# Depthwise convolution of a conformer layer: taps shared out anew over four engines, input weights in chunks of 128 features with their gates

## The reference, cut to what matters

```python
def conformer_conv(h, w_pw1, b_pw1, w_dw, b_dw, ln_g, ln_b, w_pw2, b_pw2):
    a, gate = jnp.split(h @ w_pw1 + b_pw1, 2, axis=-1)      # 1024 -> 2 x 1024
    u = a * jax.nn.sigmoid(gate)
    dw = lax.conv_general_dilated(                          # 31 taps, causal, per feature
        u, w_dw[:, None, :], window_strides=(1,), padding=((CONV_WIDTH_2 - 1, 0),),
        dimension_numbers=('NWC', 'WIO', 'NWC'), feature_group_count=D_MODEL) + b_dw
    ...                                                     # layer norm of dw, silu
    return z @ w_pw2 + b_pw2
```

## Time and profile before

| what | us |
|---|---|
| median of 3 runs | 1363.0 |
| lowest and highest run | 1354.35, 1363.15 |
| the profiled execution's own time | 1360.02 |
| its span in the trace | 1358.2 |
| PE busy in the span | 1295.7 (95%) |
| DVE busy | 920.8 (68%) |
| ACT busy | 712.7 (52%) |
| POOL busy | 43.3 (3%) |

### The profile page before, as it was taken

The page is one execution under the profiler, slowest core; times in us unless marked ns, Lnnn a source line. Parts: engine busy times, 40 slices in busy tenths (PEclk is TensorE's granted clock), DMA queues, the critical chain, the costliest instruction groups (busy, mean ns, idle before and its releaser), DMA issues.

```text
span 1358.2 us, 17587 instructions
## 1 busy us (share of the span) xinstructions
PE 1295.7 (95%) x7034; PEld 1106.1 (81%) x7034; DVE 920.8 (68%) x1270; ACT 712.7 (52%) x1074; POOL 43.3 (3%) x80
## 2 busy tenths in 40 slices
PE   6999999999999878999999999999998998999997
PEld 5998678888888767888888877888888996788886
DVE  4967565676666676666667756666666895776665
ACT  5865344554445654555445544544446664544443
POOL 0000000000000400000000000000000000000000
PEclk9999999999999889999999999999999998999999
DMA  6453235455555311455555543555554321455551
GB/s 241 156 186 124 94 110 200 155 187 187 186 186 169 143 62 47 144 213 186 187 186 187 198 152 126 184 186 189 187 188 166 109 79 62 155 187 186 202 186 62
DMA packets 30785, 215.17 MB, mean 158 GB/s; under 512 B 3552, under 2 KB 3808, under 8 KB 5488
## 3 DMA queue, kind: packets, MB, share of 16 engines
q1 hardware_dynamic: 30704, 214.05, 44.0%
HBM read 212.99 MB, written 1.05 MB: 158 GB/s over the span
## 4 chain that ended last, share of the span: by engine, by line
PE 89%; DVE 5%; ACT 3%; issue 1%; POOL 0%; DMA 0%; SPq 0%; POOLq 0%; ACTq 0%; DVEq 0%
PE pb L428 24%; PE pb L399 15%; PE pb L401 14%; PE pb L400 14%; PE pb L430 12%; PE pb L913 3%; PE pb L405 2%; DVE wlo L1432 2%; ACT arena L980 1%; DVE arena L1436 1%; ACT both L980 1%; DVE both L1445 1%; PE pb L754 1%; ACT whi L976 1%; PE pb L531 0%
## 5 line engine op out<-in xcount | busy, mean ns | idle before, releaser
L1432 DVE TENSOR_TENSOR wlo<-raw,whi 128x2048 fp32r<-128x2048 f32 (+2 forms) x201 | 453.3, 2272 | 233.8 <-ACT whi L976 233.7
L428 PE MATMUL pb<-both,whi 128*128 128x512 f32 x1408 | 498.4, 398 | 6.5 <-DVE both L1445 4.3
L976 ACT ACTIVATE whi<-raw 128x2048 fp32r<-128x2048 f32 (+2 forms) x201 | 379.3, 1893 | 39.9 <-PE pb L401 35.6
L430 PE MATMUL pb<-both,wlo 128*128 128x256 f32 x1408 | 394.9, 280 | 0.0
L428 PEld LDWEIGHTS pb<-both,whi 128*128 128x128 f32 x1408 | 264.4, 188 | 73.3 <-issue 5.1
L399 PE MATMUL pb<-whi,both 128*128 128x512 f32 (+1 forms) x754 | 298.0, 395 | 11.2 <-DVE both L1445 5.3
L401 PE MATMUL pb<-whi,both 128*128 128x512 f32 (+1 forms) x754 | 294.1, 390 | 0.0
L400 PE MATMUL pb<-wlo,both 128*128 128x512 f32 (+1 forms) x754 | 293.5, 389 | 0.0
L430 PEld LDWEIGHTS pb<-both,wlo 128*128 128x128 f32 x1408 | 265.8, 189 | 1.4
L980 ACT ACTIVATE arena<-pb 128x256 f32<-128x256 f32 (+1 forms) x248 | 103.5, 426 | 252.1 <-PE pb L430 171.8
L399 PEld LDWEIGHTS pb<-whi,both 128*128 128x128 f32 x754 | 142.7, 189 | 44.7 <-issue 8.6
(11 more groups left out here) (117 smaller groups left out, 913.6 us busy)
## 6 DMA issues: line engine op xcount, KB each, us to landing
raw<-d_ws SPq DMA_DIRECT2D x196, 1024.0 KB, 4.9
raw<-d_ws SPq DMA_DIRECT2D x3, 768.0 KB, 4.3
arena<-d_c SPq DMA_DIRECT2D x1, 1060.0 KB, 4.8
xt<-d_x SPq DMA_DIRECT2D x2, 512.0 KB, 4.2
arena<-d_rows SPq DMA_DIRECT2D x2, 512.0 KB, 5.2
out<-arena SPq DMA_DIRECT2D x2, 512.0 KB, 2.6
raw<-d_ws SPq DMA_DIRECT2D x1, 640.0 KB, 3.8
c<-d_c SPq DMA_DIRECT2D x1, 385.0 KB, 5.4
```

Source lines behind the costliest of these rows:

```text
L428: e.matmul(b[:, :], wh[:, k, fs], both[:, k, :], start=k == 0, stop=k == 7, skip_group_check=True)
L430: m = e.matmul(b[:, 256:512], wl[:, k, fs], ahi[:, k, :], start=False, stop=k == 7, skip_group_check=True)
L976: e.activation(whi[:, n % NH, 0:width(n)], raw[:, n % NR, 0:width(n)], ACT.Copy).then_inc(*sig("act.hi", f"hi{n}"))
L1432: e.tensor_tensor(wlo[:, n % NH, 0:width(n)], raw[:, n % NR, 0:width(n)], f32(whi[:, n % NH, 0:width(n)]), ALU.subtract).then_inc(*sig("dv ...
```

## The change

- The `pw1` weights are laid out by the host so that each chunk p holds 128 values and the 128 gates that belong to them. Tile p can be gated as soon as chunk p is done; the sigmoid, the gating and tap 0 are done tile by tile.
- The 30 other taps of a tile are shared by three: PE 6, 7, 8, 8, 8, 8, 11, 15 (71 in all), DVE 15, 13, 12, 12, 12, 12, 10, 10 (96) and a third share of 9, 10, 10, 10, 10, 10, 9, 5 (73). For these, ACT makes the product `up * w` (128x256, SBUF to SBUF): the first of a tile into `part` (three buffers), the others into `prod` (`NX` = 6 buffers), and POOL adds each `prod` to `part` (65 tensor-tensor adds, both inputs in SBUF, each waiting for the one before). DVE adds `part` to `cv` (`add_part`, 8 of them).
- DVE works on tile p - 1 (first `FIRST` taps) and on the rest of tile p - 2, alternating; `add_part(p - 3)` and `add_taps(p - 3)` end each round. PE's `taps(p - 1)` follow chunk p.
- ACT's order in a round is: sigmoid, `hi`, tap 0, three products, the diagonals, the other products. A product waits for the sum six products before it. The turn of the first quarter (`turn(0)`) comes before the four output banks are claimed.

```diff
--- before.py
+++ after.py
@@ -70,8 +70,7 @@
     plan += [("w_ukv", 0, 2, 1024 * j, 1024) for j in range(2)]
     plan += rows("w_o", 4) + ffn("1")
     plan += moving("ret_w_in", 0, 2560) + rows("mix_w_out", 4)[2:] + rows("mix_w_out", 4)[:2] + ffn("2")
-    for j in range(4):
-        plan += stationary("pw1", 256 * j, 256) + stationary("pw1", 1024 + 256 * j, 256)
+    plan += stationary("pw1", 0, 2048)
     plan += rows("pw2", 4) + ffn("3")
     return plan
 
@@ -266,8 +265,13 @@
         return self.c2[:, a:a + n]
 
 
-ON_PE = (12, 12, 12, 12, 12, 12, 17, 17)
+ON_PE = (6, 7, 8, 8, 8, 8, 11, 15)
+ON_DVE = (15, 13, 12, 12, 12, 12, 10, 10)
+FIRST = (9, 7, 6, 6, 6, 6, 5, 10)
+ON_POOL = tuple(30 - a - b for a, b in zip(ON_PE, ON_DVE))
 NG = 12
+NX = 6
+AHEAD = 1
 
 
 class ConfTiles:
@@ -281,6 +285,8 @@
         self.bst = room(24)
         self.mv = room(4)
         self.diag = room(128 * NG, NG)
+        self.part = room(256 * 3, 3)
+        self.prod = room(256 * NX, NX)
 
 
 SSD_UNITS = [(c, g, hh) for c in range(2) for g in range(2) for hh in range(2)]
@@ -906,7 +912,7 @@
                 tap = [0]
 
                 def taps(ft):
-                    b = claim(f"tp{ft}", keep=True)
+                    b = claim(f"tp{ft}")
                     e.wait_ge(*at(f"up{ft}"))
                     for w in range(31 - ON_PE[ft], 31):
                         e.wait_ge(*at(f"dg{tap[0]}"))
@@ -922,17 +928,14 @@
                         m = tr(b[:, 128 * i:128 * i + 128], T.cv[:, 4 * c + i, 128 * t:128 * t + 128])
                     m.then_inc(*sig(key, f"lnT{t}{c}"))
 
-                for p in range(10):
-                    if p < 8:
-                        stationary(key, CHUNK["pw1", p], claim(f"p1.{p}"), f"p1m{p}", 6 if p == 0 else None)
-                    if p == 8:
+                for p in range(8):
+                    stationary(key, CHUNK["pw1", p], claim(f"p1.{p}"), f"p1m{p}", 6 if p == 0 else None)
+                    if p == 7:
                         stats_of(0, 0)
                         stats_of(1, 0)
-                    if p >= 2:
-                        taps(p - 2)
-                    if p in (4, 6, 8, 9):
-                        for ft in ((p - 4, p - 3) if p < 9 else (6, 7)):
-                            ring.kept.discard(spots[f"tp{ft}"])
+                    if p:
+                        taps(p - 1)
+                taps(7)
                 for t in range(2):
                     stats_of(t, 1)
 
@@ -945,9 +948,9 @@
                             m = tr(b[:, 256 * i + 128 * t:256 * i + 128 * t + 128], T.dn[:, t, 128 * ft:128 * ft + 128])
                     m.then_inc(*sig(key, f"ctm{j}"))
 
+                turn(0)
                 bs = open_out(6)
                 ring.over = (0, 1, 2, 3)
-                turn(0)
                 for j in range(4):
                     if j < 3:
                         turn(j + 1)
@@ -1361,7 +1364,7 @@
                     e.wait_ge(*at(f"r6.{t}"))
                     run(key, f"conf.xn{t}0", T.dn[:, t, 0:512], xt[:, t, 0:512], ACT.Copy, scale=st[:, 4 + t:5 + t])
                 fill_x(key, 6, "mixer_norm_g", 8)
-                tap = [0]
+                tap, made = [0], [0]
 
                 def diagonals(ft):
                     for w in range(31 - ON_PE[ft], 31):
@@ -1370,25 +1373,42 @@
                         run(key, f"dg{tap[0]}", T.diag[:, tap[0] % NG, :], ident, ACT.Copy, scale=col("w_dw", 8 * w + ft))
                         tap[0] += 1
 
-                for p in range(10):
+                def products(ft, a, b):
+
+                    for i in range(a, min(b, ON_POOL[ft])):
+                        w = 1 + ON_DVE[ft] + i
+                        if i == 0:
+                            if ft >= 3:
+                                e.wait_ge(*at(f"part.gone{ft - 3}"))
+                            run(key, f"part{ft}", T.part[:, ft % 3, :], T.up[:, ft, w:w + 256], ACT.Copy,
+                                scale=col("w_dw", 8 * w + ft))
+                            continue
+                        if made[0] >= NX:
+                            e.wait_ge(*at(f"summed{made[0] - NX}"))
+                        run(key, f"prod{made[0]}", T.prod[:, made[0] % NX, :], T.up[:, ft, w:w + 256], ACT.Copy,
+                            scale=col("w_dw", 8 * w + ft))
+                        made[0] += 1
+
+                def gate(ft):
+                    e.wait_ge(*at(f"p1m{ft}"))
+                    if ft >= 2:
+                        e.wait_ge(*at(f"up{ft - 2}"))
+                    run(key, f"sg{ft}", T.sg[:, ft % 2, :], bank(f"p1.{ft}")[:, 256:512], ACT.Sigmoid,
+                        bias=col("b_pw1", 8 + ft))
+
+                for p in range(9):
+                    if p:
+                        gate(p - 1)
                     if p < 8:
                         hi(CHUNK["pw1", p] + 2)
-                    if p >= 2:
-                        diagonals(p - 2)
-                    if p < 8 and p % 2:
-                        e.wait_ge(*at(f"p1m{p}"))
-                        for i in range(2):
-                            ft = p - 1 + i
-                            if p > 1:
-                                e.wait_ge(*at(f"up{ft - 2}"))
-                            run(key, f"sg{ft}", T.sg[:, i, :], bank(f"p1.{p}")[:, 256 * i:256 * i + 256], ACT.Sigmoid,
-                                bias=col("b_pw1", 8 + ft))
-                        tally.value[f"p1.{p}.gone"] = at(f"sg{p}")
-                        for i in range(2):
-                            ft = p - 1 + i
-                            e.wait_ge(*at(f"up{ft}"))
-                            run(key, f"tap0.{ft}", T.cv[:, ft, :], T.up[:, ft, 0:256], ACT.Identity, scale=col("w_dw", ft),
-                                bias=col("b_dw", ft))
+                    if p:
+                        e.wait_ge(*at(f"up{p - 1}"))
+                        run(key, f"tap0.{p - 1}", T.cv[:, p - 1, :], T.up[:, p - 1, 0:256], ACT.Identity,
+                            scale=col("w_dw", p - 1), bias=col("b_dw", p - 1))
+                        if p < 8:
+                            products(p - 1, 0, 3)
+                        diagonals(p - 1)
+                        products(p - 1, 3 if p < 8 else 0, 31)
 
                 def turn(j):
                     e.wait_ge(*at(f"ctm{j}"))
@@ -2025,6 +2045,25 @@
                     stt(key, [f"dwt{ft}"], T.cv[:, ft, :], T.up[:, ft, w:w + 256], col("w_dw", 8 * w + ft), T.cv[:, ft, :],
                         ALU.mult, ALU.add)
 
+                def taps(p, a, b):
+
+                    new = [(p, w) for w in range(1, 1 + FIRST[p])] if p < 8 else []
+                    old = [(p - 1, w) for w in range(1 + FIRST[p - 1], 1 + ON_DVE[p - 1])] if p else []
+                    for i in range(a, min(b, max(len(new), len(old)))):
+                        for part in (old, new):
+                            if i < len(part):
+                                tap(*part[i])
+
+                def gated(ft):
+                    e.wait_ge(*at(f"sg{ft}"))
+                    stt(key, [f"up{ft}", f"p1.{ft}.gone"], T.up[:, ft, 30:286], bank(f"p1.{ft}")[:, 0:256], col("b_pw1", ft),
+                        T.sg[:, ft % 2, :], ALU.add, ALU.mult)
+
+                def add_part(ft):
+                    e.wait_ge(*at(f"sum{ft}"))
+                    e.wait_ge(*at(f"dwt{ft}"))
+                    tt(key, [f"dwt{ft}", f"part.gone{ft}"], T.cv[:, ft, :], T.cv[:, ft, :], T.part[:, ft % 3, :], ALU.add)
+
                 def add_taps(ft):
                     e.wait_ge(*at(f"tpm{ft}"))
                     e.wait_ge(*at(f"dwt{ft}"))
@@ -2034,40 +2073,24 @@
                     e.wait_ge(*at(f"lnT{t}{c}"))
                     e.bn_stats(T.bst[:, 12 * t + 6 * c:12 * t + 6 * c + 6], bank(f"ln{t}{c}")[:, :]).then_inc(*sig(key))
 
-                for p in range(10):
+                for p in range(9):
+                    if p:
+                        gated(p - 1)
+                        taps(p - 1, 0, AHEAD)
                     if p < 8:
                         lo(CHUNK["pw1", p] + 2)
+                    if p:
+                        taps(p - 1, AHEAD, 31)
                     if p == 8:
                         stats_of(0, 0)
                         stats_of(1, 0)
-                    if p < 8 and p % 2:
-                        e.wait_ge(*at(f"p1m{p - 1}"))
-                        for i in range(2):
-                            ft = p - 1 + i
-                            e.wait_ge(*at(f"sg{ft}"))
-                            stt(key, [f"up{ft}"] + ([f"p1.{p - 1}.gone"] if i else []), T.up[:, ft, 30:286],
-                                bank(f"p1.{p - 1}")[:, 256 * i:256 * i + 256], col("b_pw1", ft), T.sg[:, i, :], ALU.add,
-                                ALU.mult)
-                    if p in (4, 6, 9):
-                        pair = {4: (0, 1), 6: (2, 3), 9: (4, 5)}[p]
-                        add_taps(pair[0])
-                        add_taps(pair[1])
```

(35 more changed lines are left out.)

## The result

The changed kernel takes 1372.4 us (median of 7 runs, 1370.2 to 1378.9), the kernel before in the same runs 1361.1 (1354.4 to 1363.2): a ratio of 1.0095, 95% interval 1.0077 to 1.0114. So it is slower by 11 us, clear of the noise. The prediction's centre was 1378; the 1% that it drew as the line between a change and none is 13.6 us, and by that line the result still counts as no change, a case to which it gave 0.35.

A forecast was written before the change was run, and what follows sets the result against it. TensorE bounded the 93.3 us stretch; VectorE and GpSimd taking turns would need 100.8 us from the first tap at 1042.8, ending at 1143.6 against 1127.5, +16: 1360.0 + 16 = 1376, given as 1378 for the median, range 1350 to 1396.

The forecast's parts named there:

- a case to which it gave 0.35: Whole kernel: no change over 1% (13.6 us), 0.10 from the forecast plus 0.25 from turns costing less.
- The signs named for it: Stretch: GpSimd adds near 1 us, taps well over 0.40, TensorE gaps awaiting the gated tile, round near 13, last `add_taps` near 1143.
- the signs against it: Stretch: taps paced 0.40, gapless TensorE, last `add_taps` near 1112; or granted clock under 0.8; or ScalarE awaiting sums every round.
- the third rival: Stretch: TensorE's clock falls too; if it stays low, rounds of 18 us, 1395 and over; chance 0.10 with upper bound.
- TensorE's gain of 15 us: Stretch: 35 taps fewer on TensorE at 0.43 us, 15.1 us less if TensorE stayed the bound.
- the case that no engine excludes another: Stretch: short taps and adds slip past one another, rounds 9.4 us, 1346 up to 1350 us; chance 0.15.
- the sum: First tap to last add: VectorE's and GpSimd's excluding work in turns, plus half-hidden and waiting terms, together 100.8 us.
- the prediction's low bound: Stretch: only streaming is exclusive, tap 0.30 and GpSimd add 0.56, all else hidden; 82.3 us, -2 us.
- Half of the gatings, `add_taps` and moments: Stretch, VectorE: 7.3 us of these can have GpSimd adds beside them, so only half, 3.7 us, counts.
- The moved turn: After the stretch: `turn(0)` waits for the normalised values as before, priced at nothing; earlier bank claim at most 0.5 us.
- The rival that the turns cost less: Stretch: VectorE's and GpSimd's starts hide under each other's work, -2 to +13, 1360 to 1375 us; chance 0.25.
- TensorE stays the bound: Stretch: exclusion bites only on long instructions or short ones slip past, rounds 9.4 us, 1346 up to 1350; chance 0.15.

The follow-up runs named there:

- the PSUM version: Changed kernel with VectorE's tap sums in a PSUM bank instead of SBUF, and each tile finished one round earlier: 1345.6 us, ratio 0.9887 to the kernel before.
- the two runs: Changed kernel with GpSimd's 65 adds replaced by memsets, 1353.5 us in one run; and with VectorE's tap sums in PSUM, tiles finished one round earlier, 1345.6 us.

## Why the prediction was right

The direction, the mechanism and the place were right. The signs named for it are there: GpSimd's adds with a mean of 966 ns, taps paced 0.83, a round of 12.88 us, the last `add_taps` at 1141.4; and of the signs against it, ScalarE waiting for sums is absent. Two need a word. TensorE does wait, six times in the stage, but directly for ScalarE's diagonals and only through them for the gated tile. And the granted clock fell under 0.8 for parts of the stretch, which had been named as a sign of the third rival (see below). The time, 1372.4, is 6 us under the forecast; the measured change, +11, is 0.7 of the +16. It lies at the lower end of the forecast's own 1370 to 1388; that it is near the middle of the whole 1350 to 1396 says little, since that range spans several cases.

- *TensorE's gain of 15 us is there and not used.* TensorE had gaps of 12.3 us in 49.1. Where taps and adds do not exclude each other (the PSUM version) the stretch is 12.0 us shorter than before, against the 14 named for the case that no engine excludes another.
- *Prices that held.* ScalarE's product was put at 0.42 us and is 0.41 (7 in 2.89); GpSimd's undisturbed add at 0.74 and is 0.735; the round at 12.8 to 13.6 and is 12.88; the last add's end at 1143.6 and is 1141.8. For the last two it is in part luck: the errors in the next two points cancel.
- *The pair of tap and add was mis-sized*: 0.40 + 0.60 = 1.00 in the sum, measured 0.87. As an estimate from the earlier trace rows and the prediction's low bound, the streaming of both is 256 x 1.05 ns + 256 x 2.18 ns = 0.83, and 0.04 more is measured; so of both starts nearly all is hidden under the other's turn. That is close to the low bound's price (0.30 + 0.56). The sum had 65 x 0.13 = 8.5 us too much.
- *Two terms were too low.* Half of the gatings, `add_taps` and moments was taken as beside GpSimd's adds. In fact GpSimd has done its nine adds by then and waits for products (3.2 to 3.5 us before each of rounds 3 to 7), so nothing is hidden: 3.7 us. And in each of rounds 2 to 8 VectorE waits 0.28 us for tap 0, in all 2.0. In sum 8.5 - 3.7 - 2.0 = 2.8 us too much; predicted from the first tap 100.8, measured 98.0 (1043.81 to 1141.8). The parts were fitted to this trace after the fact; what the runs show by themselves are the 0.87, the waits of 0.28 and the total.
- *The moved turn was priced at nothing*, because it "waits for the normalised values there as before". It waited for two more of them. That step was wrong, and measured alone it is 2.8 us in the tail. Together, for the two profiled executions: 16, less 2.8 for the sum and 2.7 for the shorter tail, plus 1.0 by which the stage began later, is 11.5, of the 11.7 measured.
- *The clock* did fall: it was granted at 0.91 in the mean of rounds 2 to 6 and at 0.64 from 1129.6 to 1139.0, near the 1.2 GHz level for part of the time. In the 5 us from 1105 TensorE was busy for 2.53 us at 0.65, and the next 5 ran at 0.67; yet from 1090 it was busy for 1.53 of 5 and the clock stayed at 1.00, there and in the next 5. It cost nothing in the stretch: the chain from the first tap at 1043.81 to the last `add_taps` at 1141.40 has no piece of TensorE. So the clock of the third rival came, for part of the time, but not its longer time; its own sum for that case (a round of 9.2 + 3, still under 13) had said so. Its price for a clock that stays low has a slip: 30 us over the forecast's 1378 is 1408, not 1395.
- *The rival that the turns cost less* had -2 to +13, the forecast +10 to +25; +11 lies where both meet, so the time alone cannot choose between them. The stretch alone, +13.3, and the 14.3 us by which the last add came later are nearer the forecast's 16; the price of a pair, near the streaming alone, is the rival's. *TensorE stays the bound* did not happen; the point from which it would decide, a tap that loses less than 0.15 us, was far: a tap lost 0.47.

The Trainium skill, "SBUF — State Buffer", section "Who interferes with whom", states more than the prediction used: that a VectorE instruction with two SBUF inputs is in the way only of a GpSimd instruction that reads SBUF, and one with a single SBUF input, outside the two-port modes, is in the way of none. By this rule a memset and a sum in PSUM should both free the taps; the two runs agree (ten taps in 4.04 us, eight in 3.22). Where the prediction took "fully blocks" from that section, the runs give a smaller price: 0.87 us for a pair of short instructions, not the 0.40 + 0.735 of each alone.

## What to carry to other kernels

Before work that reads SBUF is given to GpSimd, count it and VectorE's instructions with two SBUF inputs as one engine: here an add on GpSimd took 0.47 us from VectorE, more than the tap (0.40) that it relieved it of, so a third engine that fitted by itself (nine adds of 0.82 in a round of 9.4) made the round 12.9. If one of VectorE's two inputs can stand in PSUM at the same price, the two engines run side by side, and here the same split gained 1.1% where it had lost 0.95%. And claims of buffers are waits too: look what a turn has to wait for through the banks that are claimed ahead of it.

## What the runs showed of the hardware that was not expected

- Short instructions of the two engines that exclude each other alternate one by one, with hardly any loss beside their streaming: 0.87 us for a pair of 256 columns each and 0.60 with 128 on GpSimd, some 0.04 to 0.05 over the sum of the two streams. Their starts overlap with the other's turn.
- A scalar-tensor-tensor that reads and writes its sum in PSUM has the pace of one in SBUF, 0.40 us for 256 columns.
- A GpSimd memset (312 to 316 ns in all 65 cases) is neither held by a VectorE low part of 2.28 us nor holds it.
